# Six norms and a modulation: half rows in four column groups, a power over two columns, and the second tile finished half by half

## What is computed

```python
def _layernorm(x, g, b):
    mu = jnp.mean(xf, axis=-1, keepdims=True)
    var = jnp.mean(jnp.square(xf - mu), axis=-1, keepdims=True)
    y = (xf - mu) * lax.rsqrt(var + LN_EPS)
    return (y * g.astype(jnp.float32) + b.astype(jnp.float32)).astype(x.dtype)
...
    for l in range(DEPTH):
        h = _swiglu(x, ffn_w1[l, 0], ffn_w3[l, 0], ffn_w2[l, 0])
        x = _layernorm(ALPHA * x + 0.5 * h, ln_g[l, 0], ln_b[l, 0])
        h = _mixer(x, l, w_in[l], gate_b[l], ...)
        x = _layernorm(ALPHA * x + h, ln_g[l, 1], ln_b[l, 1])
        h = _swiglu(x, ffn_w1[l, 1], ffn_w3[l, 1], ffn_w2[l, 1])
        x = _layernorm(ALPHA * x + 0.5 * h, ln_g[l, 2], ln_b[l, 2])
...
        mod = jax.nn.silu(c) @ w_mod[layer] + b_mod[layer]
        mod_c = jax.nn.silu(c_ctx) @ w_mod[layer] + b_mod[layer]
        sh1, sc1, g1, sh2, sc2, g2 = jnp.split(mod[:, None, :], N_MOD, axis=-1)
        h = modulate(rmsnorm(x, norm1_g[layer]), sh1, sc1)
```

## Time and profile before

| | |
|---|---|
| median of the runs (3) | 1730.06 us (1729.62 to 1731.22) |
| the profiled execution | 1734.61 us, span 1732.9 us |
| PE busy | 1720.6 us, 99% of the span |
| DVE busy | 1145.7 us, 66% |
| ACT busy | 861.3 us, 50% |
| POOL busy | 231.0 us, 13% |
| share of PE in the chain that ended last | 91% |

### The profile page before, as it was taken

How to read it: one execution, slowest core, us unless ns; L and a number is a source line. 1 busy time by engine, 2 the same in 40 slices (tenths; PEclk the granted TensorE clock), 3 DMA queues, 4 the chain that set the end, 5 groups by cost and what they waited for, 6 DMA issues and landing times.

```text
span 1732.9 us, 31049 instructions
## 1 busy us (share of the span) xinstructions
PE 1720.6 (99%) x12693; PEld 1579.1 (91%) x12693; DVE 1145.7 (66%) x1815; ACT 861.3 (50%) x1412; POOL 231.0 (13%) x291
## 2 busy tenths in 40 slices
PE   9999999999999999999999999999999999999999
PEld 9998798999899879998799998999877888979999
DVE  5774658786667566754677777666665747765553
ACT  5444354674444435443544754454436446555543
POOL 2000042221000000000132212000012515210000
PEclk9999999999999999999999999999999999999999
DMA  8676577445657657765676445777535434466653
GB/s 277 220 246 216 180 244 233 153 144 189 204 192 255 222 171 250 255 209 194 209 234 217 134 160 170 248 238 243 177 118 172 103 93 131 146 194 195 195 189 104
DMA packets 257518, 334.71 MB, mean 193 GB/s; under 512 B 15210, under 2 KB 217168, under 8 KB 257376
## 3 DMA queue, kind: packets, MB, share of 16 engines
q1 hardware_dynamic: 251312, 317.42, 56.4%
q0 software_dynamic: 6064, 15.31, 2.7%
HBM read 327.45 MB, written 1.05 MB: 190 GB/s over the span
## 4 chain that ended last, share of the span: by engine, by line
PE 91%; DVE 4%; DMA 2%; ACT 1%; issue 1%; POOL 0%; SPq 0%; POOLq 0%; DVEq 0%; ACTq 0%
PE bank L757 19%; PE bank L760 19%; PE bank L758 19%; PE bank L801 7%; PE bank L802 7%; PE bank L799 7%; DVE wlo L2013 2%; PE bank L923 1%; ACT whi L1571 1%; DMA mtmp<-mtmp 1%; PE bank L773 1%; PE bank L1049 1%; PE bank L883 1%; PE bank L777 1%; PE bank L781 1%
## 5 line engine op out<-in xcount | busy, mean ns | idle before, releaser
L2013 DVE TENSOR_TENSOR wlo<-raw,whi 128x1024 fp32r<-128x1024 f32 x549 | 669.8, 1228 | 335.3 <-ACT whi L1571 331.2
L1571 ACT ACTIVATE whi<-raw 128x1024 fp32r<-128x1024 f32 x549 | 572.1, 1051 | 405.8 <-PE bank L802 217.3
L757 PE MATMUL bank<-XTh,whi 128*128 128x256 f32 x1984 | 555.6, 280 | 0.0
L760 PE MATMUL bank<-XTh,wlo 128*128 128x256 f32 x1984 | 551.6, 278 | 0.5 <-DVE wlo L2013 0.5
L758 PE MATMUL bank<-XTl,whi 128*128 128x256 f32 x1984 | 551.0, 278 | 0.0
L760 PEld LDWEIGHTS bank<-XTh,wlo 128*128 128x128 f32 x1984 | 374.6, 189 | 1.5 <-DVE wlo L2013 1.4
L757 PEld LDWEIGHTS bank<-XTh,whi 128*128 128x128 f32 x1984 | 372.8, 188 | 2.3
L758 PEld LDWEIGHTS bank<-XTl,whi 128*128 128x128 f32 x1984 | 372.9, 188 | 0.0
L757 PE MATMUL bank<-HCh,whi 128*128 128x256 f32 (+2 forms) x864 | 244.3, 283 | 0.0
L758 PE MATMUL bank<-HCl,whi 128*128 128x256 f32 (+2 forms) x864 | 242.2, 280 | 0.0
L760 PE MATMUL bank<-HCh,wlo 128*128 128x256 f32 (+2 forms) x864 | 242.1, 280 | 0.0
(11 more groups left out here) (370 smaller groups left out, 2367.4 us busy)
## 6 DMA issues: line engine op xcount, KB each, us to landing
raw<-in_ffn_w_dram SPq DMA_DIRECT2D x131, 1024.0 KB, 5.2
raw<-in_w_in_dram SPq DMA_DIRECT2D x76, 1024.0 KB, 5.2
raw<-in_w_mod_dram SPq DMA_DIRECT2D x24, 1024.0 KB, 5.1
raw<-in_w_branch_dram SPq DMA_DIRECT2D x16, 1024.0 KB, 5.0
raw<-in_w_out_dram SPq DMA_DIRECT2D x12, 1024.0 KB, 5.0
raw<-in_w_ffn_gate_dram SPq DMA_DIRECT2D x11, 1024.0 KB, 5.1
raw<-in_w_ffn_up_dram SPq DMA_DIRECT2D x11, 1024.0 KB, 5.1
raw<-in_w_ffn_down_dram SPq DMA_DIRECT2D x8, 1024.0 KB, 5.0
```

The lines of the kernel that those rows point to most:

```text
L757: e.matmul(o, hi[:, k, w0:w0 + nc_], xh, start=first and k == 0, stop=False)
L760: m = e.matmul(o, lo[:, k, w0:w0 + nc_], xh, start=False, stop=last and k == nk - 1)
L1571: e.activation(hi_part(n), raw_part(n), ACTF.Copy).then_inc(WHI.did(n), 1)
L2013: e.tensor_tensor(lo_part(n), raw_part(n), hi_part(n).bitcast(F32), ALU.subtract).then_inc(WLO.did(n), 1)
```

## The change

Four things. First, a modulation half no longer accumulates its four matmuls in two rows. Matmul k writes 32 rows at 32k of the bank, from a stationary of 32 columns of `csil` (two of use, the rest zeros or neighbours), so each of the four stands in a column group of its own. ACT copies the whole bank of 128 rows, the first half to `spare`, the second to a buffer of the feed-forward; POOL adds the two (`mod_rows`, new); `mod_columns` is now four transposes of 128x128, and DVE sums the four quarters while it reads them (`mod_turned`). The matmul with `cmb` and `cmb` itself go. The columns of group 1 move from norm 1 into the feed-forward behind it, those of group 2 from norm 3 to behind the value products of the mixer, and for group 11 both halves accumulate in the bank. Second, POOL's power reads and writes two columns (the second holds 1.0), and for the rms norms one power serves both tiles. Third, tile 1 is centred and scaled half by half, and all low parts of x and (in norm 5) the weight split come behind it. Fourth, in norms 0 and 3 the high products of tile 0 come ahead of tile 1's transposes.

```diff
             def modulation_half(g, h, first, last, b):
...
                 for k in range(4):
-                    kk = 4 * h + k
-                    m = e.matmul(bank[b][0:2, :], csil[:, kk, :], raw_whole(c)[:, k, :], start=kk == 0, stop=last and k == 3)
-                    if between and k == 1:
-                        between()
+                    m = e.matmul(bank[b][32 * k:32 * k + 32, :], csil[:, 8 * h + 2 * k:8 * h + 2 * k + 32], raw_whole(c)[:, k, :], start=first, stop=last)
...
             def mod_columns(g, b):
                 q.wait_ge(AMD, ("row", g, 1))
-                q.wait_ge(TAB, "cmb")
+                if g != 11:
+                    q.wait_ge(PLN, ("rows", g))
                 empty(b)
                 for j in range(4):
-                    e.matmul(bank[b][:, 2 * j:2 * j + 2], spare[0:2, j * 128:(j + 1) * 128], cmb[0:2, :], start=True, stop=True)
-                settle(b).then_inc(MOD.did(("columns", g)), 1)
+                    m = e.transpose(bank[b][:, j * 128:(j + 1) * 128], spare[:, j * 128:(j + 1) * 128], ident)
+                m.then_inc(MOD.did(("columns", g)), 1)
...
                 modulation_half(g, h, True, True, row_bank(j))
-                if turn:
+                if turn and j % 3:
                     turn_x(j + 1, 1)
-                    if h:
-                        mod_columns(g, row_bank(j))
-                    elif j % 3:
-                        empty(2)
-                        settle(2)
+                    empty(2)
+                    settle(2)
...
+            def mod_turned(g, b):
+                q.wait_ge(MOD, ("columns", g))
+                parts_of = bank[b][:, :].rearrange("p (a j r) -> p a r j", a=4, j=4)
+                e.tensor_reduce(modc[:, 4 * g:4 * g + 4, :], parts_of[:, :, 0:2, :], AX.X, ALU.add).then_inc(DMD.did(g), 1)
...
-                center(1)
-                if j % 3 == 0:
-                    low_x(j + 1, 0, 0)
-                scale(1)
+                moments(1)
+                for c in range(2):
+                    center(1, slice(c * 512, c * 512 + 512))
+                    scale(1, c)
                 w.more(1)
+                if not turn:
+                    w.more(1)
                 w.take_whole()
...
             def unit_rows(j, src, t, at):
-                q.wait_ge(P2, ("unit", j, t))
+                q.wait_ge(P2, ("unit", j))
...
             def layernorm(j):
                 for t in range(2):
                     q.wait_ge(DLN, ("var", j, t))
-                    e.tensor_tensor(rs[:, t, 1:2], rs[:, t, 0:1], nhalf, ALU.pow).then_inc(PLN.did(("rs", j, t)), 1)
+                    e.tensor_tensor(rs[:, t, 2:4], rs[:, t, 0:2], half[:, 0:2], ALU.pow).then_inc(PLN.did(("rs", j, t)), 1)
+
+            def mod_rows(g):
+                q.wait_ge(AMD, ("row", g, 1))
+                e.tensor_tensor(spare[:, :], spare[:, :], mod_rows_of(g, 1)[:, :], ALU.add).then_inc(PLN.did(("rows", g)), 1)
...
             def second():
-                for t in range(2):
-                    unit_rows(0, t, 6 + t)
+                unit_rows(0, 6)
+                mod_rows(7)
```

More of the change, by code:

```diff
@@ L783, in gemm_pair, with gemm_b @@
                     m.then_inc(MM.did(("w", n)), 1)
-            def gemm_b(name, nparts, nk, X, tiles, banks, width, ready=None, tail=4, between=None, head=1):
+            def gemm_b(name, nparts, nk, X, tiles, banks, width, ready=None, tail=4, between=None, head=1, turn_second=None):
                 def product(n, p, ti, c, *names):
@@ L908, in modulation, with modulation_half @@
                 emptied[b] = ((DMD, g),)
-            def modulation_half(g, h, first, last, b, between=None):
+            def modulation_half(g, h, first, last, b):
                 c = w.take_whole()
@@ L1004, in mixer @@
                 ready = x_ready(s)
-                gemm_b(("V", l), 8, 1, xt_b, (0, 1), [[4, 5], [6, 7]], 1024, lambda k, t, halves=None: ready(k, halves, (t,)), tail=3, head=2)
+                gemm_b(("V", l), 8, 1, xt_b, (0, 1), [[4, 5], [6, 7]], 1024, lambda k, t, halves=None: ready(k, halves, (t,)), tail=3, head=2,
+                       turn_second=lambda: turn_x(s, 1))
                 for b in range(4, 8):
                     emptied[b] = ((AMX, ("V", l, (b - 4) // 2, b % 2)),)
-                empty(3)
-                settle(3)
+                if l:
+                    mod_columns(2, 3)
+                else:
+                    empty(3)
+                    settle(3)
                 for n in range(16):
@@ L1583, in mod_row @@
                 q.wait_ge(MOD, ("mod", g, h))
-                if g in ROW_BEFORE:
-                    q.wait_ge(MOD, ("columns", ROW_BEFORE[g]))
-                e.activation(spare[0:2, :], bank[b][0:2, :], ACTF.Copy).then_inc(AMD.did(("row", g, h)), 1)
+                if h == 0 or g == 11:
+                    if g in ROW_BEFORE:
+                        q.wait_ge(MOD, ("columns", ROW_BEFORE[g]))
+                e.activation(mod_rows_of(g, h)[:, :], bank[b][:, :], ACTF.Copy).then_inc(AMD.did(("row", g, h)), 1)
             def ffn_up(i, at):
@@ L2021, in sum_up @@
                     q.wait_ge(MOD, ("columns", BEFORE[g]))
+                if (g, h) == (3, 0):
+                    q.wait_ge(PLN, ("rows", 1))
                 for k in (2 * step, 2 * step + 1):
@@ L2088, in center, with scale @@
                     e.tensor_scalar(rs[:, t, 0:1], mv[:, t, 1:2], LN_EPS, None, ALU.add).then_inc(DLN.did(("var", j, t)), 1)
-                    xa = X[:, t, :]
                     q.wait_ge(GB, gbn)
-                    e.scalar_tensor_tensor(xa, xa, mv[:, t, 0:1], gb[:, 0, :], ALU.subtract, ALU.mult).then_inc(DLN.did(("g", j, t)), 1)
-                def scale(t):
-                    if t and not turn:
-                        w.more(1)
+                def center(t, cols):
+                    xv = X[:, t, cols]
+                    e.scalar_tensor_tensor(xv, xv, mv[:, t, 0:1], gb[:, 0, cols], ALU.subtract, ALU.mult).then_inc(DLN.did(("g", j, t)), 1)
+                def scale(t, c):
+                    xv = X[:, t, c * 512:(c + 1) * 512]
                     q.wait_ge(PLN, ("rs", j, t))
                     q.wait_ge(DLN, ("g", j, t))
-                    for c in range(2):
-                        xv = X[:, t, c * 512:(c + 1) * 512]
-                        e.scalar_tensor_tensor(xv, xv, rs[:, t, 1:2], gb[:, 1, c * 512:(c + 1) * 512], ALU.mult, ALU.add).then_inc(
-                            DLN.did(("x", j, t, c), ("x", j, t)), 1)
+                    e.scalar_tensor_tensor(xv, xv, rs[:, t, 2:3], gb[:, 1, c * 512:(c + 1) * 512], ALU.mult, ALU.add).then_inc(
+                        DLN.did(("x", j, t, c), ("x", j, t)), 1)
                 for c in range(2):
@@ L2105, in layernorm @@
                     stats(0, c)
-                center(0)
+                moments(0)
+                center(0, slice(0, D))
                 add(1, 0)
-                scale(0)
+                scale(0, 0)
+                scale(0, 1)
                 stats(1, 0)
@@ L2135, in mixer @@
                 w.more(3)
+                if l:
+                    mod_turned(2, 3)
                 def stats_v(t):
@@ L2340, in context @@
                     unit_squares(1, t, 2 + t)
+                for t in range(2):
                     unit_rows(1, CX, t, 2 + t)
@@ L2844, in gpsimd @@
                 if l:
-                    for t in range(2):
-                        unit_rows(1, t, 2 + t)
+                    unit_rows(1, 2)
                 layernorm(3 * l + 2)
```

84 lines of the change are left out of this document (46 added, 38 removed).

## The result

The changed kernel takes 1760.83 us (median of 4 runs, 1760.02 to 1764.64) against 1730.64 us for the kernel before, a ratio of 1.0174 [1.0150 to 1.0197]. It is 30 us slower; 6 were forecast, and the range ended at 1741. A repetition in another job gave 1759.69 against 1733.31 us, 1.0153 [1.0127 to 1.0179].

What follows compares the result with a forecast made beforehand. TensorE, busy 99% of the span, was taken as the bound. Chains +2.8 and clock falls +3.5 gave +6.3 us on the 1730.06 median: 1736.4 us, range 1725 to 1741.

Steps and rivals of the forecast that it cites:

- The chains: Sequences of dependent engine work in the six norms and the end; their changes were summed to +2.8 us.
- Norm 3: Low x products 0.94 us earlier, less 0.8 for POOL's addition holding DVE; moved columns counted separately at +0.5 less 0.1.
- not in size (0.50 of 0.74): On the skill's SBUF lock-out rule: DVE lost only 0.50 us beside a 0.74 us POOL addition.
- Norm 5: Low products wait for later weight splits, then columns wait for POOL's sum: +1.9 us, bounds +0.7 and +2.4.
- end: End of second block: high part up to 0.5 us earlier, four transposes for columns another 0.5: -1.0 us.
- the 2.5 us times eight are mostly turned into idle time: Shorter modulation halves save TensorE 2.5 us in eight places, but it then mostly waits for DVE.
- Busy PE down by some 20 us: Sign expected in the profile after: TensorE's busy time some 20 us lower while the span grows.
- I charge 1.5 for norm 5 and 0.4 for each of the other five: Clock term: falls of the granted clock around norms and end add 3.5 us, bounds 0 and 9.9.
- no extra fall of the clock: Rival, chance 0.20: only the chains count, +2.8 us, 1732.9 us.
- The point from which this decides: Norm 5 threshold: fourth weight split done by 1281 instead of 1283.9, and the addition by the low products' end.
- the faster case: Rival, chance 0.20: TensorE's shorter list also decides norm 5, ending it 4.0 us earlier; in all -6.8, 1723.3 us.
- POOL holds nobody: Rival, chance 0.15: two-column power unhindered and addition slips between DVE's work: -1.4, 1728.7 us.

Runs made afterwards that it cites:

- e1: Changed kernel with the four matmuls of each modulation half accumulated in one column group, so a half takes 3.5 us again: 1748.57 us, 1.0099.
- e10: The kernel before, unchanged, run again for a second trace: 1730.36 us.
- e3: Changed kernel without POOL's addition; eight matmuls with the identity add the two half rows in the bank: 1756.69 us, 1.0132.
- e4: Changed kernel with tile 1 centred as a whole, then scaled in two halves; two-column power kept: 1755.10 us, 1.0121.
- e6: Changed kernel with tile 1 centred whole, one-column power, a low x part and norm 5's weight split back in its shadow; halves stay short: 1751.11 us, 1.0113.
- e14: Changed kernel plus seven two-column matmuls and one identity transpose behind the columns of group 11: 1756.26 us, 1.0124.
- e11: The kernel before, unchanged, run again for a third trace: 1736.35 us.

## Why the prediction was wrong

**The chains were nearly right.** Starts and ends behind the start of tile 0's transposes, in us:

| | before | after | at full clock | predicted step |
|---|---|---|---|---|
| tile 1 scaled, norm 2 | 5.11 | 5.61 | 5.62 (e1) | +0.45 |
| tile 1 scaled, norm 1, with the addition | 5.13 | 6.48 | | 0.45 + 0.8 |
| low-weight products, norm 2 | 7.99 | 9.71 | 8.50 (e1) | +0.45 |
| low-weight products, norm 1 | 9.43 | 10.28 | 8.46 (e1) | -0.97 |
| low x products, norm 0 | 8.08 | 8.99 | 8.57 (e1) | +0.4 |
| low x products, norm 3 | 9.44 | 9.85 | 9.63 (e1) | -0.94 + 0.8 |

Norm 3 is the one that missed: a gain of 0.14 was forecast, and e1 has a loss of 0.19 at full clock, since the addition there holds the weight splits and TensorE waits for them. The power over two columns ended 0.55 us behind the half centring (0.56 predicted). The halves overlapped as the pair of column halves had let expect: 1.07 us by the row with its tail. The estimate from "TensorE: Matmul & The Clock Gate", Part 3, of the Trainium skill was 0.9, and the trace agrees within 0.2, tail counted. POOL's addition held DVE for 1.64 - 0.75 = 0.89 us (0.8 taken) in norm 1 and, in e1, for 3.44 - 2.35 = 1.09 of its 1.43 us. By "SBUF: two separate sides" of "SBUF — State Buffer" in the Trainium skill the one of such a pair that starts first keeps the other out until it ends. The trace agrees within 0.2 us: when the scaling began, 1.08 us of the addition were left (456.53 to 457.61), and it lost 0.89; the splits in e1 had 1.22 before them and lost 1.09. The prediction's "not in size (0.50 of 0.74)" set the loss against the whole addition instead of the 0.63 us that were left of it when the subtraction began.

*Norm 5*, from the last down product to the products behind the columns, took 11.52 us before and 13.16 after: +1.6 with part of it at 0.50, and +1.3 in e1, where 1.9 was predicted. The low products waited for the splits and the columns for POOL, as told. The *end*, from the first half of group 11 to the products behind the columns, went from 18.34 to 18.48, both with work at 0.50 in it: +0.1 instead of -1.0. Without a fall it is 17.46 in e10 and 16.74 in e1, -0.7. TensorE's idle time grew by 21.6 us: "the 2.5 us times eight are mostly turned into idle time" was right too. "Busy PE down by some 20 us" was not: it grew by 4.2.

e1's trace, which has all chains of the change and no fall in a norm, is the nearest thing to their sum. Its span is 3.0 us above before; with the clock (0.1) and some 105 matmuls fewer at 118 ns (0.5) taken out, 3.4, and +2.8 was forecast.

**The step that failed is the clock**: "I charge 1.5 for norm 5 and 0.4 for each of the other five (one in two falls, half of it beside waits): +3.5". The trace has 17.2 us, beyond even the 9.9 of its bound. Some 1.65 of the 17.2 belong to the fall at 1334.9, which the change did not make; with 15.5 left the rest of the argument stands. Each part of the quoted sentence is wrong. Not one norm in two had a fall, but all six in both traces of the changed kernel, and four or five in e3, e4, e6 and e14, whose halves are short too. Not half of it beside waits: TensorE was busy 37.5 of 40.0 us. And a fall is not always 3.3 us: norms 3, 4 and 5 and the end had 6.7. The waits themselves were forecast (2.1 and 1.0 us in norm 1, measured 2.17 and 1.68). The end was forecast to gain with waits of over 2 us in it.

The row that the chance was taken from, one fall behind one wait of 2.3 us, could not have told this. In the two later traces of the kernel before the same place has waits of 2.29 and 1.92 us, and the clock stays at 1.00 behind both. In e10:

```profile
1534.30 0.70 PE L1497 MATMUL bank<-QNT,nm 128*128 128x256 f32 x2 [2.29 <-POOL QNT L2823]
...
1534.30:1540.00 5.70, 5.70 (x14) 1.23 (x14) 4.45 (x8) 2.10 (x6) 0.00 (x0) 1.00 0.34 90
```

One chance in two was not far off for that place. In norms 1, 2 and 4 a second wait of 0.3 to 1.7 us follows 0.7 us behind the first, and there the clock fell in 11 of 12 cases (four traces: two of the changed kernel, e3 and e14). That is what the chance of one half left out.

**A term that the sum did not have** is the pitch, +10.1 us between the two traces. By the two traces more of the kernel before it is partly chance (2213, 2691 and 3180 at 118 ns; the changed kernel 4928 and 4268); how much of it the change brings, and by what, stays open. The wait in the second mixer, +2.0 us, was not foreseen either.

Of the rivals, "no extra fall of the clock" is refuted. "The point from which this decides" of the faster case, the fourth split done by 1281, was not reached. "POOL holds nobody" fell with the 1.64 us of the scaling.

For the chains I had +2.8. What clock and pitch leave for them in the changed kernel is 25.8 - 17.2 - 10.1 = -1.5. Against e1's +3.4 that is too little by 4.9 us, and a reason can be argued: half of the busy time charges all work at 0.50 to the clock, and some of it filled time in which TensorE would have waited anyway. No run parts the two further. So the clock's share is known to some 5 us: between 12 and 17 of the 25.8.

## What to carry to other kernels

Work that TensorE does while it waits for another engine is not only free, it can hold the clock: here 2.5 us of it taken away in eight places (20 us) came back as 21.6 us of idle time, and the work behind ran 12 to 17 us slower. Before such an edit, look in several traces for waits of the length that the edit would make and see how often the granted clock fell behind them; one trace showed one fall here, and two others of the same kernel none at that place. Where the edit makes two waits close together, put the fall of every such place into the range, with two stretches of low clock for some of them, and charge it on the work that follows. When the chain of the waiting engine cannot be shortened as well, leave the cover where it is.

## What the runs showed of the hardware

- Dense streams of 256-column matmuls run at 113 or at 118 ns each at a granted clock of 1.00, for whole stretches. The first feed-forward, behind the same instructions, stood at 118 in both traces of the changed kernel and at 113 in e1 and e4; of the kernel before it stood at 113 in two traces and at 118 in one (e10):

```profile
20.00:50.00 30.00, 30.00 (x267) 30.00 (x266) 17.88 (x23) 16.45 (x23) 1.62 (x3) 1.00 0.80 250
```

  (e1, against 257 records in the changed kernel). In some places the speed changed across two or four transposes; The last feed-forward, 1187 matmuls or 5.3 us between the two speeds, ran wholly or mostly at 118 in 12 of the 15 traces of kernels with transposed columns and in one of three of the kernel before. What picks the speed stays open.
- A wait of 2.2 us followed by one of 0.3 to 1.7 brought the clock to 0.50 in 11 of 12 norms, but not in norm 2 of e3, with the same waits as norm 2 of the changed kernel. In norm 0, where the high products stand between shorter waits (1.1 and 0.8 us), it fell in both traces of the changed kernel and not in e3 and e14. So the same waits may or may not lose it.
- The clock also fell without any wait. In 13 of the 18 traces it went to 0.50 some 19 to 20 us behind the transposes of x in the second block, in the kernel before in e11 alone. What TensorE did before it there were eight records with 32 partitions instead of 128, without a gap:

```profile
1308.71 3.93 PE L1232 MATMUL bank<-SO 32*128 32x512 f32 x8
...
1312.10:1315.30 3.20, 3.20 (x13) 2.73 (x13) 2.55 (x4) 1.81 (x3) 0.00 (x0) 0.50 0.37 143
```

  The same records stand in the five traces without the fall; why it falls there was not tried.
